# The third output-matrix unit of each MLP's last quarter computed by block products

## The chip, the cores and the metric

One Trainium2 chip, one core. The metric is the device time of one launch in microseconds (us), the median of several runs. The kernel has one long program: TensorE (PE) multiplies, VectorE (DVE), ScalarE (ACT) and GpSimd (POOL) prepare operands and take results, SyncE (SP) loads weights.

## The reference, cut to what matters

A first block (gated delta net, retention, a gated MLP) is followed by two layers of attention and a squared-relu MLP on a hidden state of 512 tokens by 1024 features, all in float32. The change touches the two MLPs of those layers and the norms behind them:

```
h = h + mix                                  # 512 x 1024
n = rms_norm(h, norm_mlp_g[i])               # over the 1024 features
h = h + relu(n @ w_in) ** 2 @ w_out          # w_in 1024 x 4096, w_out 4096 x 1024
# behind layer 0: rms_norm(h, norm_mix_g[1]), then n @ b_w_qkv
# behind layer 1: rms_norm(h, norm_final_g), the result
```

## The kernel before

**Tiles.** The hidden state is kept turned: `hT` holds 8 tiles of 128 features by 512 tokens. A weight unit is 256 columns of a weight matrix over 1024 rows (1 MB); its product with 8 operand tiles gives two tiles of output. Every number is split in a rounded part and a rest (`w_hi`, `w_lo`; `n_hi`, `n_lo`; `ff_hi`, `ff_lo`), and every product is three: hi by hi, hi by lo, lo by hi (`products`, lines 1063 to 1065). A plain unit is therefore 2 x 8 x 3 = 48 matmuls of 512 columns. SP loads a unit into one half of `raw` (line 898) as soon as the unit two before it has its rests; ACT makes its rounded part (`split_hi`, line 1895), DVE its rest (`split_lo`, line 1901).

**Quarters.** An MLP is done in four quarters m (0 to 3 in layer 0, 4 to 7 in layer 1) of 1024 inner features: four units of the input matrix, then four of the output matrix (units 0 to 3 of `p_dn[m]`), each of which is added to two tiles of `hT` (`residual_group`, line 3196): unit 0 to tiles 0 and 1, unit 1 to 2 and 3, unit 2, the third, to 4 and 5, unit 3 to 6 and 7.

**Block products.** The input units of quarters 1 to 3 are computed by a scheme of seven products of half-size blocks in place of eight (`block_tensor`, `piece_product`, lines 1500 to 1502): 7 x 4 x 3 = 84 matmuls of 256 columns. The pieces are A11, A12, A22, S2, S3, S1, S4 in this order; the S pieces are sums of weight blocks (made by `paired_sums`, `second_sum`, `fourth_sum`), the T factors are sums of operand blocks. In quarters 1, 2, 5 and 6 (`has_down`) the third output unit, called DOWN, is also done so. DVE then makes its weight sums behind the last input unit (`burst_vector`) and four operand sums in `scratch` (`down_sums`); ACT and DVE split these (`t_split_high`, `t_split_low`), and DVE adds the banks to tiles 4 and 5 in eight steps (`first_added`, `third_added`, `second_added`, `last_added`, lines 2141 to 2160), of which the steps wait for pieces S2, S3, S1 and S4. In quarters 3 and 7 all four output units are plain: `project` on PE, `rounds` on ACT, `residual` on DVE.

**The norms behind quarters 3 and 7** (n = 5 and n = 7). ACT reads the tiles of `hT` in three parts (tiles 0 to 3, 4 and 5, 6 and 7). For n = 5, `input_part` makes the rounded operands `n_hi` of a part (line 2232) and its squares in `scratch` (line 2223), and between part 0 and part 1 ACT splits the first weight unit of layer 1 (`next_split`). DVE makes the rests `n_lo` (`low`, line 2361), the rest of that weight unit (line 1901) and the residual additions. POOL adds the squares of the parts (`norm_pool`, lines 987, 989, 990), each step when the part's squares are there. For n = 7, the last, DVE multiplies the tiles by the norm's weights (`weighted`, line 2334) in place of the rests, and adds tile 6's squares to POOL's sum (line 2352) before it adds the last tile 7 (line 2343); then PE sums over features, DVE and ACT make the roots and scale the turned rows (`x_rows`), and SP stores them.

**What sets the order.** Each engine runs its own list in the order in which it is written. Engines wait for each other by counting semaphores. DVE's list behind quarter 3 is: rests of tiles 0 to 3, addition of tiles 4 and 5, rests of 4 and 5, rest of the next weight unit, additions and rests of 6 and 7. PE's first matmul of layer 1's projection waits for the rest of that weight unit.

Of the kernel before, what the change touches and what calls it, by code (L numbers as in the profile page):

```python
# [18 lines left out]
KD = D // P  # L19
# [186 lines left out]
def build(nc, t, out):  # L206
# [15 lines left out]
    with ctx:  # L222
# [543 lines left out]
        BLOCKS, DOWN = UNITS + 1, UNITS  # L766
        PIECES = [(name, u) for u in range(BLOCKS) for name in FACTORS]
        PIECE_AT = {piece: n for n, piece in enumerate(PIECES)}
# [3 lines left out]
        SPLITS = [(op, u) for u in range(UNITS) for op in ("A1", "S23", "S14")]  # L772
        SPLITS += [(op, DOWN) for op in ("T4", "T2", "A1", "S23", "T3", "S14", "T1")]
        SPLIT_AT = {op: n for n, op in enumerate(SPLITS)}
        T_SUMS = ("T1", "T3", "T2", "T4")
        SUM_AT = [3 * u for u in range(BLOCKS)]
        OPERANDS, SUMS = 4, KD + 4

        def has_down(m):
            return m % 4 in (1, 2)  # L780

        def counted(m, each, short, begin):

            layer, quarter = divmod(m, 4)
            return layer * (begin + 2 * each + short) + (begin + (quarter - 1) * each if quarter else 0)

# [5 lines left out]

        def pieces_before(m):
            return counted(m, len(PIECES), len(FACTORS) * UNITS, 0)

        def splits_before(m):

            return counted(m, len(SPLITS), 3 * UNITS, OPERANDS) + m // 4

        def sums_before(m):  # L800

            return counted(m, 3 * BLOCKS + len(T_SUMS), 3 * UNITS, SUMS)

        def kept_before(m):
            return counted(m, BLOCKS, UNITS, 0)

        PIECE_HI_ENDS = OPERANDS + 2 * len(SPLITS) + 3 * UNITS + 1

        def split_count(m, op):
            return splits_before(m) + SPLIT_AT[op] + 1  # L810

        def piece_split(eng, m, op, u, what):

            if op == "A22":
                eng.wait_ge({"hi": hi_ready, "lo": lo_ready}[what], unit_index(m, u) + 1)
            else:
                eng.wait_ge(at("piece_" + what), split_count(m, (op, u)))

        def piece_used(eng, m, piece):
            eng.wait_ge(at("piece_used"), pieces_before(m) + PIECE_AT[piece] + 1)  # L820

        def summed(eng, m, u, n):

            eng.wait_ge(at("sums_ready"), sums_before(m) + SUM_AT[u] + n)

# [43 lines left out]
        def kept(eng, m, u):  # L869
            eng.wait_ge(at("kept"), kept_before(m) + u + 1)  # L870

# [656 lines left out]
        def burst_tensor(pe, m):  # L1528
            if m % 4 == 1:
                pe.wait_ge(at("piece_lo"), splits_before(m))  # L1530
            for u in range(UNITS):
                block_tensor(pe, m, u)
# [479 lines left out]
        def operands_high(act, m):  # L2012

            act.wait_ge(w_used, p_in[m].u0 + 4)
            act.wait_ge(at("sums_ready"), sums_before(m) + KD)
            n0 = splits_before(m + 1) - OPERANDS
            for half in range(2):
                tiles = slice(4 * half, 4 * half + 4)
                done(act, act.activation(n_hi[:, tiles, :], n_whole[:, tiles, :], ACT.Copy), at("piece_hi"), n0 + half + 1)

        def operands_high_late(act, m):
            n0 = splits_before(m + 1) - OPERANDS
            act.wait_ge(at("sums_ready"), sums_before(m) + SUMS)
            act.wait_ge(at("piece_lo"), n0 + 2)
            for half in range(2):
                tiles = slice(KD + 4 * half, KD + 4 * half + 4)
                done(act, act.activation(ff_hi[:, tiles, :], t_tiles[:, 4 * half:4 * half + 4, :], ACT.Copy), at("piece_hi"), n0 + half + 3)

        def normed(dve, m, layer):

            for f in range(KD):
                done(dve, dve.scalar_tensor_tensor(n_whole[:, f, :], hT[:, f, :], input_weight((4, 6)[layer], f), rstd[:, :], ALU.mult, ALU.mult),
                     at("sums_ready"), sums_before(m) + f + 1)

        def operand_sums(dve, m):
            near, far = near_far(n_whole)
            n0 = sums_before(m) + KD
            done(dve, dve.tensor_tensor(t_parts[:, 0], near[:, :, LATER], near[:, :, EARLY], ALU.subtract), at("sums_ready"), n0 + 1)
            done(dve, dve.scalar_tensor_tensor(t_parts[:, 1], far[:, :, LATER], -1.0, t_parts[:, 0], ALU.mult, ALU.subtract), at("sums_ready"), n0 + 2)
            done(dve, dve.scalar_tensor_tensor(t_parts[:, 2], far[:, :, LATER], -1.0, near[:, :, LATER], ALU.mult, ALU.subtract), at("sums_ready"), n0 + 3)  # L2040
            done(dve, dve.tensor_tensor(t_parts[:, 3], t_parts[:, 1], far[:, :, EARLY], ALU.add), at("sums_ready"), n0 + 4)

        def operand_low(dve, m, n):

            n0 = splits_before(m + 1) - OPERANDS
            dve.wait_ge(at("piece_hi"), n0 + n + 1)
# [4 lines left out]
            done(dve, dve.tensor_tensor(lo, whole, hi.bitcast(F32), ALU.subtract), at("piece_lo"), n0 + n + 1)  # L2051

# [26 lines left out]
        def paired_sums(dve, m, u):  # L2079
# [47 lines left out]
        def first_kept(act, m, u):  # L2127

            piece_used(act, m, ("A11", u))
            done(act, act.activation(first_row(u), unit_banks(u)[0][:, EARLY], ACT.Copy), at("kept"), kept_before(m) + u + 1)  # L2130

# [25 lines left out]
        def last_added(dve, m, u):  # L2157
            piece_used(dve, m, ("S4", u))
            row = down_rows()[0][:, LATER]
            done(dve, dve.tensor_tensor(row, unit_banks(u)[0][:, LATER], row, ALU.add), bank_free, unit_group(m, u) + 3)  # L2160

        def down_sums(dve, m):

            n0 = sums_before(m) + 3 * BLOCKS
            t1, t3, t2, t4 = (t_whole(scratch, name) for name in T_SUMS)
# [5 lines left out]
        def t_split_high(act, m, name):  # L2171

            act.wait_ge(at("sums_ready"), sums_before(m) + 3 * BLOCKS + len(T_SUMS))
            if name == "T1":
# [154 lines left out]
        def last_norm_vector(dve):  # L2329
# [35 lines left out]
        def norm_vector(dve, n):  # L2365
# [266 lines left out]
        def mlp_scalar(act, layer):  # L2632
# [17 lines left out]
            for m in range(first + 1, first + 4):  # L2650
                burst_scalar(act, m)
                if has_down(m):
                    down_scalar(act, m)
            rounds(act, p_dn[first + 3], a_own, 0, split_hi, no_group)

        def down_scalar(act, m):
# [10 lines left out]
            split_hi(act, ph.u0 + 3, 1)  # L2667
            for op in PIECE_OF_OP:
                piece_high(act, m + 1, op, 0)

# [533 lines left out]
        def mlp_vector(dve, layer):  # L3204
# [517 lines left out]
```

## Time and profile before

| | |
|---|---|
| median of 3 runs | 1871.3 us (1871.23 to 1871.88) |
| span of the profiled execution, first to last instruction | 1869.4 us |
| busy PE, DVE, ACT, POOL | 99%, 71%, 50%, 5% |
| last chain | PE 94%, DVE 3%, ACT 1%, DMA 1% |
| granted TensorE clock | 0.999 on average |

The page gives the span of the profiled execution and no other time of it; the runs' median is 1.9 us above that span. A timeline row reads: start in us, length in us, engine, line, operation, output<-inputs, shapes, count; in brackets the idle time of the engine just before and what ended it. A merged row (x2, x4) has the time of all. Matmuls overlap: their pace is the distance of their starts, not their length.

### The profile page before, as it was taken

The page shows a single profiled execution, that of the slowest core. Times are in us where ns is not written, and L with a number is a line of the kernel's source. Part 1 is how long each engine was busy: PE and PEld are TensorE (multiplying, and loading weights), DVE is VectorE, ACT ScalarE, POOL GpSimd, SP SyncE. Part 2 cuts the span into 40 slices and gives each one's busy share as a digit, 9 for nine tenths or more (in the row PEclk, how much of TensorE's full clock was granted, in tenths as well). Part 3 has the DMA queues.
Part 4 walks back from the last instruction along what each step waited for, and adds up shares of the span by engine and source line. Part 5 has one row for each costly group of instructions (what it writes and reads, how often), then busy time and mean ns, then how long its engine had stood idle before and what let it go on. Part 6 is the DMA issues. An engine that isn't in the chain of part 4 may idle for free.

```text
span 1869.4 us, 28026 instructions
## 1 busy us (share of the span) xinstructions
PE 1857.1 (99%) x10531; PEld 1541.6 (82%) x10531; DVE 1329.9 (71%) x1824; ACT 931.1 (50%) x1190; POOL 101.9 (5%) x90
## 2 busy tenths in 40 slices
PE   9999999999999999999999999999999999999998
PEld 7788878888888887877889898988778788989897
DVE  7767774677357667556577898947788658789884
ACT  6392464555133344444543554545667744445462
POOL 0010021000000021000100000020110010000001
PEclk9999999999999999999999999999999999999999
DMA  7223122322322234222232223334232133233321
GB/s 242 90 91 123 40 68 68 109 93 68 112 90 94 76 100 140 68 78 68 93 101 97 93 95 109 98 108 147 88 105 71 60 101 104 81 105 99 105 90 68
DMA packets 146801, 179.31 MB, mean 96 GB/s; under 512 B 3582, under 2 KB 140670, under 8 KB 144257
## 3 DMA queue, kind: packets, MB, share of 16 engines
q1 hardware_dynamic: 143296, 160.44, 26.2%
q0 software_dynamic: 3104, 17.10, 2.9%
q8 instruction: 72, 1.18, 0.3%
q14 instruction: 41, 0.33, 0.1%
q10 hardware_dynamic: 288, 0.26, 0.0%
HBM read 173.48 MB, written 2.20 MB: 94 GB/s over the span
## 4 chain that ended last, share of the span: by engine, by line
PE 94%; DVE 3%; ACT 1%; DMA 1%; issue 0%; SPq 0%; DVEq 0%; ACTq 0%
PE bank L1063 23%; PE bank L1065 23%; PE bank L1064 23%; PE bank L1500 5%; PE bank L1501 5%; PE bank L1502 5%; PE bank L1191 2%; PE bank L1805 2%; PE bank L1787 1%; PE bank L1197 1%; PE bank L1676 1%; PE bank L1677 1%; PE bank L1678 1%; PE bank L1611 1%; PE bank L1664 1%; DVE w_lo L1901 0%
## 5 line engine op out<-in xcount | busy, mean ns | idle before, releaser
L1063 PE MATMUL bank<-n_hi,w_hi 128*128 128x512 f32 x1054 | 425.0, 403 | 1.4 <-DVE w_lo L1901 1.3
L1065 PE MATMUL bank<-n_hi,w_lo 128*128 128x512 f32 x1054 | 417.7, 396 | 0.0
L1064 PE MATMUL bank<-n_lo,w_hi 128*128 128x512 f32 x1054 | 416.6, 395 | 0.0
L1895 ACT ACTIVATE w_hi<-raw 128x2048 fp32r<-128x2048 f32 (+2 forms) x117 | 218.8, 1870 | 371.9 <-PE bank L1065 369.3
L1901 DVE TENSOR_TENSOR w_lo<-raw,w_hi 128x2048 fp32r<-128x2048 f32 (+2 forms) x123 | 275.7, 2242 | 112.2 <-ACT w_hi L1895 110.2
L1064 PE MATMUL bank<-ff_lo,w_hi 128*128 128x512 f32 x784 | 309.0, 394 | 0.0
L1065 PE MATMUL bank<-ff_hi,w_lo 128*128 128x512 f32 x720 | 286.2, 397 | 0.0
L1063 PE MATMUL bank<-ff_hi,w_hi 128*128 128x512 f32 x720 | 284.4, 395 | 0.6 <-DVE ff_lo L2200 0.6
L1063 PEld LDWEIGHTS bank<-n_hi,w_hi 128*128 128x128 f32 x1054 | 198.0, 188 | 53.9 <-issue 5.0
L1064 PEld LDWEIGHTS bank<-n_lo,w_hi 128*128 128x128 f32 x1054 | 198.1, 188 | 48.8 <-issue 2.9
L1065 PEld LDWEIGHTS bank<-n_hi,w_lo 128*128 128x128 f32 x1054 | 197.9, 188 | 47.0
L1064 PEld LDWEIGHTS bank<-ff_lo,w_hi 128*128 128x128 f32 x784 | 147.2, 188 | 36.7 <-issue 0.7
L1063 PEld LDWEIGHTS bank<-ff_hi,w_hi 128*128 128x128 f32 x720 | 135.1, 188 | 33.8 <-DVE ff_lo L2200 1.9
L1065 PEld LDWEIGHTS bank<-ff_hi,w_lo 128*128 128x128 f32 x720 | 135.1, 188 | 32.1
L3196 DVE TENSOR_TENSOR hT<-hT,bank 128x512 f32<-128x512 f32 (+1 forms) x94 | 64.6, 687 | 95.7 <-PE bank L1065 92.9
L1500 PE MATMUL bank<-ff_hi,w_hi 128*128 128x256 f32 x432 | 122.2, 283 | 0.0
L1501 PE MATMUL bank<-ff_lo,w_hi 128*128 128x256 f32 x432 | 122.0, 282 | 0.0
L1502 PE MATMUL bank<-ff_hi,w_lo 128*128 128x256 f32 x432 | 121.1, 280 | 0.0
L2062 ACT ACTIVATE w_hi<-consts 128x1024 fp32r<-128x1024 f32 x56 | 59.4, 1062 | 98.8 <-PE bank L1065 57.4
L1502 PEld LDWEIGHTS bank<-ff_hi,w_lo 128*128 128x128 f32 x432 | 82.1, 190 | 0.0
L1500 PE MATMUL bank<-n_hi,w_hi 128*128 128x256 f32 x288 | 81.5, 283 | 0.0
L1501 PE MATMUL bank<-n_lo,w_hi 128*128 128x256 f32 x288 | 81.4, 282 | 0.0
(455 smaller groups left out, 3015.2 us busy)
## 6 DMA issues: line engine op xcount, KB each, us to landing
raw<-in_mlp_w_in SPq DMA_DIRECT2D x32, 1024.0 KB, 5.4
raw<-in_mlp_w_out SPq DMA_DIRECT2D x32, 1024.0 KB, 5.1
raw<-in_w_up SPq DMA_DIRECT2D x22, 1024.0 KB, 5.1
raw<-in_w_units SPq DMA_DIRECT2D x14, 1024.0 KB, 4.8
raw<-in_a_w_qkv SPq DMA_DIRECT2D x12, 1024.0 KB, 5.1
raw<-in_b_w_qkv SPq DMA_DIRECT2D x12, 1024.0 KB, 5.2
b_bias<-bias_table POOLq DMA_DIRECT2D x16, 448.0 KB, 4.6
raw<-in_w_down SPq DMA_DIRECT2D x8, 768.0 KB, 4.6
```

The lines of the kernel that those rows point to most:

```text
L1063: nc.tensor.matmul(b[:, :], w_hi[:, j % 2, cols], hi, start=start, stop=False)
L1064: nc.tensor.matmul(b[:, :], w_hi[:, j % 2, cols], lo, start=False, stop=False)
L1065: return nc.tensor.matmul(b[:, :], w_lo[:, j % 2, cols], hi, start=False, stop=final)
L1191: ins = nc.tensor.transpose(b[:, i * P:(i + 1) * P], src(i), ident)
L1500: nc.tensor.matmul(b, w_hi_flat[:, cols], hi[:, k, :], start=k == 0, stop=False)
L1501: before = nc.tensor.matmul(b, w_hi_flat[:, cols], lo[:, k, :], start=False, stop=False)
L1502: ins = nc.tensor.matmul(b, w_lo_flat[:, cols], hi[:, k, :], start=False, stop=k == KD // 2 - 1)
L1805: ins = nc.tensor.matmul(b[:, :], b_v[:, head, k, :], b_at[:, head % 2, k, :], start=k == 0, stop=k == TOK - 1)
L1895: act.activation(w_hi[:, s, cols], raw[:, s, cols], ACT.Copy).then_inc(hi_ready, 1)
L1901: dve.tensor_tensor(w_lo[:, s, cols], raw[:, s, cols], w_hi[:, s, cols].bitcast(F32), ALU.subtract).then_inc(lo_ready, 1)
L2062: ins = act.activation(by_rows(places(w_hi_flat, op, u), op), source(m, op, u), ACT.Copy)
L3196: ins = dve.tensor_tensor(h, h, b[:, :].unsqueeze(1), ALU.add)
```

## The change

`has_down(m)` is now true for the quarters 3 and 7 too, so their third output unit becomes a DOWN unit of seven pieces, with weight sums, operand sums, splits and additions as in quarters 1, 2, 5 and 6. The next quarter's preparations, which follow there, are left out. ACT now waits, before part 0 of the norms 5 and 7, until piece S1 is used. DVE's addition of tiles 4 and 5 is the eight-step one, and the work on tiles 0 to 3 (rests for n = 5, weighting for n = 7), formerly ahead of the addition of tiles 4 and 5, stands between its fourth and its fifth step. The semaphore counts, formerly worked out by formulas, come from tables that are filled in the order of the work; this alone changes no instruction.

```diff
         def has_down(m):
-            return m % 4 in (1, 2)
+            return m % 4 > 0
...
+        def third_unit_added(dve, m, between):
+            first_added(dve, m, DOWN)
+            third_added(dve, m, DOWN)
+            between()
+            second_added(dve, m, DOWN)
+            last_added(dve, m, DOWN)
...
             def input_part(part):
                 residual_part(act, n, part)
+                if n == 5 and part == 0:
+                    piece_used(act, 3, ("S1", DOWN))
...
             for part in range(2):
                 residual_part(act, 7, part)
+                if part == 0:
+                    piece_used(act, 7, ("S1", DOWN))
                 squared(act, 7, part)
...
             own_splits(dve, ph, split_lo)
-            weighted(0, 4)
-            residual_group(dve, ph, ph.iters - 1, 0)
+            third_unit_added(dve, 7, lambda: weighted(0, 4))
             weighted(4, 6)
...
-                low(*PARTS[0])
+                if n != 5:
+                    low(*PARTS[0])
                 own_splits(dve, ph, split_lo, ...)
-                residual_group(dve, ph, ph.iters - 1, 0)
+                if n == 5:
+                    third_unit_added(dve, 3, lambda: low(*PARTS[0]))
+                else:
+                    residual_group(dve, ph, ph.iters - 1, 0)
                 low(*PARTS[1])
                 next_split(dve, n, split_lo, 0)
                 residual_group(dve, ph, ph.iters - 1, 1)
...
                 if has_down(m):
                     down_scalar(act, m)
-            rounds(act, p_dn[first + 3], a_own, 0, split_hi, no_group)
...
                 if has_down(m):
                     down_vector(dve, m)
-            residual(dve, p_dn[first + 3])
...
             piece_low(dve, m, "S14", DOWN)
             t_split_low(dve, m, "T1")
             split_lo(dve, ph.u0 + 3, 1)
+            if m % 4 == 3:
+                return
             first_added(dve, m, DOWN)
```

## Rows read from the trace of the kernel before

**Rows 1.** The page: busy us and share; granted clock in 40 slices.

```profile
PE 1857.1 (99%) x10531; PEld 1541.6 (82%) x10531; DVE 1329.9 (71%) x1824; ACT 931.1 (50%) x1190; POOL 101.9 (5%) x90
...
PEclk9999999999999999999999999999999999999999
```

**Rows 2.** Timeline of PE: first matmuls of three units, plain ones before and behind.

```profile
1236.00 0.40 PE L1063 MATMUL bank<-ff_hi,w_hi 128*128 128x512 f32 x1
...
1258.40 0.40 PE L1063 MATMUL bank<-n_hi,w_hi 128*128 128x512 f32 x1
...
1834.90 0.39 PE L1063 MATMUL bank<-ff_hi,w_hi 128*128 128x512 f32 x1
```

**Rows 3.** Timeline of PE: first matmul of quarter 6's DOWN and unit 3.

```profile
1750.77 0.28 PE L1500 MATMUL bank<-ff_hi,w_hi 128*128 128x256 f32 x1
...
1760.94 0.44 PE L1063 MATMUL bank<-ff_hi,w_hi 128*128 128x512 f32 x1
```

**Rows 4.** Timeline of PE and DVE; waits of PE (us, times, longest).

```profile
1736.66 0.50 PE L1063 MATMUL bank<-ff_hi,w_hi 128*128 128x512 f32 x1 [0.65 <-DVE ff_lo L2200]
...
1732.66 1.23 DVE L2088 TENSOR_TENSOR consts<-raw 128x1024 f32<-128x1024 f32 x1 [2.54 <-DMA raw<-in_mlp_w_out]
...
PE bank L1063 <- DVE ff_lo L2200: 0.6, 1, 0.6
```

**Rows 5.** Timeline of ACT and DVE in and behind quarter 6's DOWN unit.

```profile
1752.46 0.38 ACT L2130 ACTIVATE kept_rows<-bank 128x256 f32<-128x256 f32 x1 [0.79 <-PE bank L1502]
...
1758.46 2.29 DVE L1901 TENSOR_TENSOR w_lo<-raw,w_hi 128x2048 fp32r<-128x2048 f32 x1 [0.59 <-ACT w_hi L1895]
...
1761.97 0.69 DVE L2143 TENSOR_TENSOR hT<-hT,kept_rows 128x512 f32<-128x512 f32 x1
...
1762.70 0.42 DVE L2147 TENSOR_TENSOR kept_rows<-bank,kept_rows 128x256 f32<-128x256 f32 x1
...
1767.79 0.42 DVE L2160 TENSOR_TENSOR hT<-bank,hT 128x256 f32<-128x256 f32 x1
```

**Rows 6.** Timeline of ACT, DVE and POOL, norm 5 behind quarter 3.

```profile
1238.23 3.00 ACT L2232 ACTIVATE n_hi<-hT,par 128x512 fp32r<-128x512 f32 x4
...
1240.63 3.12 DVE L2361 SCALAR_TENSOR_TENSOR n_lo<-hT,par,n_hi 128x512 fp32r<-128x512 f32 x4
...
1241.26 1.92 ACT L2223 ACTIVATE scratch<-hT 128x2048 f32<-128x2048 f32 x1
...
1249.43 1.48 ACT L2232 ACTIVATE n_hi<-hT,par 128x512 fp32r<-128x512 f32 x2
...
1250.26 1.54 DVE L2361 SCALAR_TENSOR_TENSOR n_lo<-hT,par,n_hi 128x512 fp32r<-128x512 f32 x2 [2.08 <-ACT n_hi L2232]
...
1251.83 2.29 DVE L1901 TENSOR_TENSOR w_lo<-raw,w_hi 128x2048 fp32r<-128x2048 f32 x1
...
1252.15 4.24 POOL L989 TENSOR_TENSOR scratch<-scratch 128x1024 f32<-128x1024 f32 x1 [6.14 <-ACT scratch L2223]
```

**Rows 7.** Timeline, norm 7; line 2334 by itself (min/median/max ns).

```profile
1839.14 2.62 POOL L987 TENSOR_TENSOR scratch<-scratch 128x1024 f32<-128x1024 f32 x1 [327.03 <-ACT scratch L2223]
...
1848.39 2.40 POOL L989 TENSOR_TENSOR scratch<-scratch 128x1024 f32<-128x1024 f32 x1 [6.63 <-ACT scratch L2223]
...
1850.87 1.29 POOL L990 TENSOR_TENSOR scratch<-scratch 128x512 f32<-128x512 f32 x1
...
1857.57 0.69 DVE L2343 TENSOR_TENSOR hT<-hT,bank 128x512 f32<-128x512 f32 x1 [3.35 <-PE bank L1065]
...
L2334 DVE TENSOR_SCALAR h_w<-hT,par x8: 486/487/2508, 1839.5 to 1858.3; 128x512 f32<-128x512 f32 x8
```

**Rows 8.** Timeline of POOL, and the last chain in time, in norm 2.

```profile
694.24 2.71 POOL L996 TENSOR_TENSOR a_k<-a_k,scratch 128x1024 f32<-128x1024 f32 x1 [2.00 <-ACT scratch L2223]
...
694.71 2.80 DVE a_stage L2417
```

**Rows 9.** Waits of PE: the longest one.

```profile
PE bank L1813 <- DVE g_S L3618: 1.1, 1, 1.1
```

More of the change, by code:

```diff
@@ L766, in build @@
         BLOCKS, DOWN = UNITS + 1, UNITS
-        PIECES = [(name, u) for u in range(BLOCKS) for name in FACTORS]
-        PIECE_AT = {piece: n for n, piece in enumerate(PIECES)}
         PLACE = {"A11": 0, "A12": 1, "A22": 2, "S2": 4, "S3": 5, "S1": 6, "S4": 7}
@@ L771, in build @@
         PIECE_OF_OP = {"A1": ("A11", "A12"), "A22": ("A22",), "S23": ("S2", "S3"), "S14": ("S1", "S4")}
-        SPLITS = [(op, u) for u in range(UNITS) for op in ("A1", "S23", "S14")]
-        SPLITS += [(op, DOWN) for op in ("T4", "T2", "A1", "S23", "T3", "S14", "T1")]
-        SPLIT_AT = {op: n for n, op in enumerate(SPLITS)}
         T_SUMS = ("T1", "T3", "T2", "T4")
-        SUM_AT = [3 * u for u in range(BLOCKS)]
-        OPERANDS, SUMS = 4, KD + 4
+        OPERANDS = 4
+        DOWN_SPLITS = ("T4", "T2", "A1", "S23", "T3", "S14", "T1")
         def has_down(m):
-            return m % 4 in (1, 2)
-        def counted(m, each, short, begin):
-            layer, quarter = divmod(m, 4)
-            return layer * (begin + 2 * each + short) + (begin + (quarter - 1) * each if quarter else 0)
+            return m % 4 > 0
         def unit_index(m, u):
@@ L791, in unit_group, with count @@
             return p_in[m].g0 + u if u < UNITS else p_dn[m].g0 + 2
[L793 to L810, printed above, removed]
+        piece_count, split_count, sum_count, kept_count = {}, {}, {}, {}
+        def count(table, *key):
+            table[key] = len(table) + 1
+        for layer in range(2):
+            for n in range(KD + 4):
+                count(sum_count, 4 * layer, "operand", n)
+            if layer:
+                count(split_count, 4, "output_begun")
+            for n in range(OPERANDS):
+                count(split_count, 4 * layer, "operand", n)
+            for m in range(4 * layer + 1, 4 * layer + 4):
+                for u in range(BLOCKS if has_down(m) else UNITS):
+                    count(kept_count, m, u)
+                    for name in FACTORS:
+                        count(piece_count, m, name, u)
+                    for op in DOWN_SPLITS if u == DOWN else ("A1", "S23", "S14"):
+                        count(split_count, m, op, u)
+                    for n in (1, 2, 3):
+                        count(sum_count, m, u, n)
+                if has_down(m):
+                    for name in T_SUMS:
+                        count(sum_count, m, name)
+        PIECE_HI_ENDS = split_count[4, "output_begun"]
         def piece_split(eng, m, op, u, what):
@@ L816, in piece_split @@
             else:
-                eng.wait_ge(at("piece_" + what), split_count(m, (op, u)))
+                eng.wait_ge(at("piece_" + what), split_count[m, op, u])
         def piece_used(eng, m, piece):
-            eng.wait_ge(at("piece_used"), pieces_before(m) + PIECE_AT[piece] + 1)
+            eng.wait_ge(at("piece_used"), piece_count[(m,) + piece])
         def summed(eng, m, u, n):
-            eng.wait_ge(at("sums_ready"), sums_before(m) + SUM_AT[u] + n)
+            eng.wait_ge(at("sums_ready"), sum_count[m, u, n])
         def places_free(eng, m, op, u):
@@ L869, in kept @@
         def kept(eng, m, u):
-            eng.wait_ge(at("kept"), kept_before(m) + u + 1)
+            eng.wait_ge(at("kept"), kept_count[m, u])
         def unit_rows(u):
@@ L1529, in burst_tensor @@
             if m % 4 == 1:
-                pe.wait_ge(at("piece_lo"), splits_before(m))
+                pe.wait_ge(at("piece_lo"), split_count[m - 1, "operand", OPERANDS - 1])
             for u in range(UNITS):
@@ L2014, in operands_high @@
             act.wait_ge(w_used, p_in[m].u0 + 4)
-            act.wait_ge(at("sums_ready"), sums_before(m) + KD)
-            n0 = splits_before(m + 1) - OPERANDS
+            act.wait_ge(at("sums_ready"), sum_count[m, "operand", KD - 1])
             for half in range(2):
                 tiles = slice(4 * half, 4 * half + 4)
-                done(act, act.activation(n_hi[:, tiles, :], n_whole[:, tiles, :], ACT.Copy), at("piece_hi"), n0 + half + 1)
+                done(act, act.activation(n_hi[:, tiles, :], n_whole[:, tiles, :], ACT.Copy), at("piece_hi"), split_count[m, "operand", half])
         def operands_high_late(act, m):
-            n0 = splits_before(m + 1) - OPERANDS
-            act.wait_ge(at("sums_ready"), sums_before(m) + SUMS)
-            act.wait_ge(at("piece_lo"), n0 + 2)
+            act.wait_ge(at("sums_ready"), sum_count[m, "operand", KD + 3])
+            act.wait_ge(at("piece_lo"), split_count[m, "operand", 1])
             for half in range(2):
                 tiles = slice(KD + 4 * half, KD + 4 * half + 4)
-                done(act, act.activation(ff_hi[:, tiles, :], t_tiles[:, 4 * half:4 * half + 4, :], ACT.Copy), at("piece_hi"), n0 + half + 3)
+                done(act, act.activation(ff_hi[:, tiles, :], t_tiles[:, 4 * half:4 * half + 4, :], ACT.Copy), at("piece_hi"), split_count[m, "operand", 2 + half])
         def normed(dve, m, layer):
@@ L2032, in normed @@
                 done(dve, dve.scalar_tensor_tensor(n_whole[:, f, :], hT[:, f, :], input_weight((4, 6)[layer], f), rstd[:, :], ALU.mult, ALU.mult),
-                     at("sums_ready"), sums_before(m) + f + 1)
+                     at("sums_ready"), sum_count[m, "operand", f])
         def operand_sums(dve, m):
             near, far = near_far(n_whole)
-            n0 = sums_before(m) + KD
+            n0 = sum_count[m, "operand", KD] - 1
             done(dve, dve.tensor_tensor(t_parts[:, 0], near[:, :, LATER], near[:, :, EARLY], ALU.subtract), at("sums_ready"), n0 + 1)
@@ L2043, in operand_low @@
         def operand_low(dve, m, n):
-            n0 = splits_before(m + 1) - OPERANDS
-            dve.wait_ge(at("piece_hi"), n0 + n + 1)
+            dve.wait_ge(at("piece_hi"), split_count[m, "operand", n])
             half = slice(4 * (n % 2), 4 * (n % 2) + 4)
@@ L2050, in operand_low @@
                              (t_tiles[:, half, :], ff_hi[:, spare, :], ff_lo[:, spare, :]))
-            done(dve, dve.tensor_tensor(lo, whole, hi.bitcast(F32), ALU.subtract), at("piece_lo"), n0 + n + 1)
+            done(dve, dve.tensor_tensor(lo, whole, hi.bitcast(F32), ALU.subtract), at("piece_lo"), split_count[m, "operand", n])
         def unit_loaded(eng, v):
@@ L2129, in first_kept @@
             piece_used(act, m, ("A11", u))
-            done(act, act.activation(first_row(u), unit_banks(u)[0][:, EARLY], ACT.Copy), at("kept"), kept_before(m) + u + 1)
+            done(act, act.activation(first_row(u), unit_banks(u)[0][:, EARLY], ACT.Copy), at("kept"), kept_count[m, u])
         def down_rows():
@@ L2171, in t_split_high @@
         def t_split_high(act, m, name):
-            act.wait_ge(at("sums_ready"), sums_before(m) + 3 * BLOCKS + len(T_SUMS))
+            act.wait_ge(at("sums_ready"), sum_count[m, T_SUMS[-1]])
             if name == "T1":
@@ L2667, in down_scalar @@
             split_hi(act, ph.u0 + 3, 1)
-            for op in PIECE_OF_OP:
-                piece_high(act, m + 1, op, 0)
+            if m % 4 < 3:
+                for op in PIECE_OF_OP:
+                    piece_high(act, m + 1, op, 0)
         def burst_scalar(act, m):
```

8 lines of the change are left out of this document (4 added, 4 removed).

## The prediction, written before the change was built or run

> **What bounds the kernel now.** I read the page first: PE is busy 99% of the span and its clock is at the full level, 2.4 GHz, in every slice [rows 1]. So time can be won only by fewer PE cycles, and every wait that is put on PE costs in full. Then the timeline of PE around the touched places. In quarter 3 the third plain unit starts at 1236.00 and the first matmul of layer 1's projection at 1258.40, with no idle time between [rows 2]: two units, 22.40 us, 11.20 each. Quarter 7's third unit starts at 1834.90 [rows 2]. A DOWN unit in quarter 6 takes 1760.94 - 1750.77 = 10.17 us [rows 3]. Then the other engines behind both places, because the change hands them more work just before PE needs their results.
>
> **What it removes.** 48 matmuls of 512 columns become 84 of 256: 11.20 - 10.17 = 1.03 us per quarter, 2.06 us in two. This is all there is to win, 0.11% of the span. The 0.2% that tells a change of this kernel from none is 3.7 us, out of reach on the fast side.
>
> **What it adds ahead of the unit.** DVE's weight sums now stand before the last rests of the inner features, and wait for the weights: 2.54 us in quarter 6 [rows 4]. PE then waited for `ff_lo`. It was idle 0.65; with the 0.40 of the matmul before, starts lay 1.05 apart in place of 0.23, and the first matmul behind took 0.50 for 0.40: 0.9 us lost. But that is the only one of four such quarters with idle time [rows 4]; a wait below 0.17 us would hide in the 0.40 of a matmul. I take 0.1 us per quarter and keep 0.9 as its upper end. Four operand sums, the splits, and the S sums cost nothing else: the same lists run behind the same PE work in quarter 6, and the 10.17 us contain what they cost.
>
> **What is late behind quarter 3.** Times from here on are in us behind DOWN's first matmul, 0.
> - DVE: the rest of unit 3's weights starts at 1758.46 - 1750.77 = 7.69; the first four additions end at 1762.70 + 0.42 - 1750.77 = 12.35 [rows 5].
> - ACT: a piece is 12/84 of 10.17, 1.45 us, so S1 is done at 8.72. A signal of this kind took 1752.46 - (1750.77 + 1.45) = 0.24 us [rows 5]. The new wait thus ends at 8.96. Queued behind it are four rounded tiles (3.00) and the squares (1.92) [rows 6], to 13.9. Then the next weights' rounded part, also 1.92, to 15.9, which is early enough.
> - DVE's four rests, 3.12 together or 0.78 each [rows 6], start at 12.4 and would end at 15.5.
> - POOL starts to add squares at 14.0, within the third rest (14.0 to 14.7). What then happens stands in the trace of norm 2: POOL's addition of the same size came at 694.24, during one vector operation on two SBUF tensors; the next one, started at 694.71, took 2.80 us in place of 0.76, and ended 0.56 behind POOL's end at 696.95 [rows 8]. The other way round, POOL's addition at 1252.15 took 4.24 us for 2.40, as DVE's split of weights had begun at 1251.83 [rows 6, 7]. So each waits for the other's whole instruction. Here POOL goes at 14.7, ends at about 17.0, and the fourth rest ends at 17.55, not 15.5: +2.05.
> - The last four additions are 0.42 + 0.69 + 0.69 + 0.42 [rows 5] with 0.03 between them: to 19.9.
> - ACT's tiles 4 and 5 start at 20.0; DVE's rests of them end 1251.80 - 1249.43 = 2.37 later [rows 6], at 22.35; the weights' rest takes 2.29, to 24.7.
> - PE ends unit 3 at 10.17 + 0.04 + 11.20 = 21.4 and needs that rest: idle to 24.75, and 0.1 for the first matmul, as above.
>
> Before, PE got there at 22.40. Net: 0.1 + 24.75 + 0.1 - 22.40 = **+2.55 us**. Without the meeting of POOL and DVE: +0.5. With no wait at all: 0.1 + 21.4 - 22.4 = -0.9. Layer 1's later waits: its first operands 6 and 7 are needed 36 matmuls (8.4 us) behind that start, and come about 5 us behind it; I take 0.
>
> Of the meeting, the Trainium skill, "SBUF — State Buffer", section "SBUF: two separate sides", says that the port pair which VectorE and GpSimd share is an exclusive lock for a whole instruction, taken also by a vector operation with two SBUF inputs against a GpSimd one that reads SBUF. The rows of norm 2 agree. It speaks against this change, because before it POOL's additions fell into gaps of DVE, and now they meet a full list.
>
> **What is late at the end (quarter 7).** The same list up to 8.96. ACT squares at once, to 10.9; POOL starts at 11.0 and runs 2.6 [rows 7], to 13.65. DVE's third addition has two SBUF inputs and would start at 1761.97 - 1750.77 = 11.2 [rows 5]; blocked, it ends at about 14.15, not 11.9: +2.25. The fourth ends at 14.6. Four weightings, 0.49 each alone (one of the eight took 2.51, started during POOL's addition [rows 7]), 2.1 in all, to 16.7. Last additions to 19.05. Squares of tiles 4 and 5 (1.07, half as many as a 128x2048 row and its start) to 20.2; POOL's additions 2.40 and 1.29 [rows 7] with about 0.5 between and before them, to 24.4, the weighting of tile 6 locked out meanwhile; DVE's addition of tile 6's squares, 0.7, to 25.2. Only then tile 7 is added. Before, this was at 1857.57 - 1834.90 = 22.67 [rows 2, 7]. Everything behind it is unchanged. Net: 0.1 + 25.2 - 22.67 = **+2.65 us**. Without the first lock: +0.4. With no wait: PE ends at 21.4, tile 7's addition 0.27 behind it as before: -0.9.
>
> **Sum.** 2.55 + 2.65 = +5.2 us on the span, 1869.4 + 5.2 = 1874.6. The profiled execution shows no more than its span; the runs' median lies 1.9 above it, and I leave that as it is: 1871.3 + 5.2 = **1876.5 us**.
>
> **The rivals.**
> - *All of it is hidden (faster).* The waits of ACT and DVE end before PE needs them. Two times -0.9: 1869.5. For it: in quarters 1, 2, 5 and 6 longer lists are hidden. Against it: there unit 3 is followed by pieces prepared earlier, here by a weight rest that stands at the end of DVE's list; even without locks I find it 1.2 us late. 5%.
> - *The lists are late, but POOL and DVE don't meet.* If POOL's addition fell between instructions, or DVE went first: 0.5 + 0.4 = +0.9, 1872.2. The gaps decide: in quarter 7 POOL comes 0.2 us ahead of the addition that it blocks. 15%.
> - *One meeting only:* 0.5 + 2.65 or 2.55 + 0.4, about +3.1, 1874.4. 20%.
> - *The idle time also costs clock (more slower).* PE would be idle 3.3 us behind quarter 3 and 3.8 us near the end, against 1.1 us at the longest before [rows 9], where the clock stayed full [rows 1]. If it fell to 1.2 GHz, a stretch as long as the idle one would run at half pace: half of 3.3, and some of the 4 us of transposes at the end, +2 to +3, 1879. No row shows such a fall before the last instructions. 15%.
> - *The waits for weights repeat* as in quarter 6, twice 0.8 more: 1878.1. In the range of the forecast.
>
> Beside the fourth rival: the Trainium skill, "TensorE: Matmul & The Clock Gate", section "Part 1: The HAM clock gate", holds that an idle TensorE drops to 1.2 GHz and is brought back by work. No run here shows it for idle stretches of this length; by it the fourth rival's time would come out.
>
> **How the numbers follow.** Forecast, both meetings at full clock: 45%, 1875.2 to 1878.3 by its own terms. The range to 8 in 10 reaches from 1872.0 (the rival without meetings, nearly) to 1879.2 (clock). Faster by over 0.2% has no mechanism: 1%. Slower by over 0.2%, above 1875.0: the forecast, the clock's case, and part of the single meeting: 63%. The same: 36%.
>
> **What would show it.** Right: PE idle about 3.3 us ahead of the first line-1063 matmul of layer 1, released by DVE's line 1901; one vector operation of 2.5 to 3 us during each of POOL's first additions (a rest, line 2361, in norm 5; line 2143 in norm 7); tile 7's last addition released not by PE but by POOL's sum; DOWN units of 10.2 us. Wrong: no idle time of PE ahead of layer 1, or POOL's additions at 2.4 us beside vector operations at 0.69 to 0.76. If the locks are there and the total is still near 1872, the error is in where the lists end.

## The result and the profile after

| | before | after |
|---|---|---|
| median of 4 runs each | 1871.6 us | 1880.75 us (1879.75 to 1881.9) |
| ratio | | 1.0046, 95% interval 1.0032 to 1.0060 |
| span of the profiled execution | 1869.4 us | 1877.9 us |

The change costs 9.2 us. The forecast was +5.2 with a range to 1879.2; the result lies 1.5 above the range. The profiled execution is 8.5 longer, and that difference can be placed. The page after, as in [rows 1]: busy time of PE and POOL, and the granted clock by fortieths of the span.

```profile
PE 1862.2 (99%) x10603; PEld 1549.7 (83%) x10603; DVE 1369.3 (73%) x1864; ACT 944.3 (50%) x1206; POOL 101.9 (5%) x90
...
PEclk9999999999999999999999999999999999999998
```

The shares tell nothing of the loss: PE is busy 99% as before. A first sign is the mean granted clock, 0.996 in this execution (0.995 to 0.998 in the four) where before had 0.999.

**Quarter 3.** Timelines of DVE and then POOL of the kernel after (start, duration, engine, line, operation, shape, then in brackets idle time and releaser). DOWN's first matmul is at 1236.25 here.

```profile
1248.65 5.15 DVE L2366 SCALAR_TENSOR_TENSOR n_lo<-hT,par,n_hi 128x512 fp32r<-128x512 f32 x4
...
1255.74 0.42 DVE L2155 TENSOR_TENSOR hT<-bank,hT 128x256 f32<-128x256 f32 x1
1257.09 1.54 DVE L2366 SCALAR_TENSOR_TENSOR n_lo<-hT,par,n_hi 128x512 fp32r<-128x512 f32 x2 [0.92 <-ACT n_hi L2236]
1258.66 2.29 DVE L1899 TENSOR_TENSOR w_lo<-raw,w_hi 128x2048 fp32r<-128x2048 f32 x1
```

```profile
1250.31 2.94 POOL L985 TENSOR_TENSOR scratch<-scratch 128x1024 f32<-128x1024 f32 x1 [336.06 <-ACT scratch L2225]
```

The four rests took 5.15, where they took 3.12 before [rows 6]. POOL's addition lies inside them, and ends at 1253.25. All that follows on DVE is 2.03 later, down to the weight rest that PE needs. PE's own timeline there:

```profile
1257.46 0.39 PE L1063 MATMUL bank<-ff_hi,w_lo 128*128 128x512 f32 x1
1261.00 0.50 PE L1061 MATMUL bank<-n_hi,w_hi 128*128 128x512 f32 x1 [3.16 <-DVE w_lo L1899]
1261.34 0.40 PE L1062 MATMUL bank<-n_lo,w_hi 128*128 128x512 f32 x1
...
1262.68 0.63 PE L1061 MATMUL bank<-n_hi,w_hi 128*128 128x512 f32 x1
1263.11 0.63 PE L1062 MATMUL bank<-n_lo,w_hi 128*128 128x512 f32 x1
...
1265.67 0.41 PE L1062 MATMUL bank<-n_lo,w_hi 128*128 128x512 f32 x1
1265.92 0.39 PE L1063 MATMUL bank<-n_hi,w_lo 128*128 128x512 f32 x1
```

The first matmul of layer 1 starts 24.75 behind DOWN's, released by the weight rest; 3.16 us of PE are idle. Then comes what the prediction's sum did not have. From 1262.68 to 1265.67 seven matmuls start 0.43 apart, not 0.23, and last 0.63, not 0.40: 7 x 0.19, and 0.17 on the one ahead of them, 1.5 us. That is the lower clock level, 1.2 GHz. The rows of stretches say the same (us, busy time and count of PE, PEld, DVE, ACT, POOL, then the granted clock):

```profile
1236.00:1261.00 25.00, 21.85 (x134) 19.09 (x132) 22.47 (x25) 14.31 (x14) 4.97 (x2) 1.00 0.27 85
1261.00:1266.00 5.00, 5.00 (x15) 3.94 (x16) 3.98 (x5) 3.43 (x4) 4.92 (x5) 0.66 0.67 216
```

While PE is idle the row shows a full clock; it is lower only behind it. The page's fortieths, 47 us each, show 9 in every one but the last: a fall of 3.4 us (1262.28 to 1265.67) cannot be seen there.

**The end (quarter 7).** Timelines of DVE, POOL and PE after. DOWN starts at 1839.13.

```profile
1850.33 2.78 DVE L2138 TENSOR_TENSOR hT<-hT,kept_rows 128x512 f32<-128x512 f32 x1
...
1859.83 2.16 DVE L2340 TENSOR_SCALAR h_w<-hT,par 128x512 f32<-128x512 f32 x1
1863.19 0.69 DVE L2357 TENSOR_TENSOR scratch<-scratch 128x512 f32<-128x512 f32 x1 [1.21 <-POOL scratch L988]
1863.92 0.69 DVE L2348 TENSOR_TENSOR hT<-hT,bank 128x512 f32<-128x512 f32 x1
...
1868.43 0.17 DVE L2359 TENSOR_REDUCE r_cols<-bank 128x4 f32<-128x8 f32 x1 [3.30 <-PE bank L1873]
```

```profile
1850.16 2.41 POOL L985 TENSOR_TENSOR scratch<-scratch 128x1024 f32<-128x1024 f32 x1 [333.79 <-ACT scratch L2225]
...
1859.33 2.38 POOL L987 TENSOR_TENSOR scratch<-scratch 128x1024 f32<-128x1024 f32 x1 [6.76 <-ACT scratch L2225]
```

```profile
1864.03 1.84 PE L1869 MATMUL bank<-consts,scratch 128*128 128x1 f32 x8 [3.33 <-DVE scratch L2357]
...
1866.62 1.71 PE L1873 MATMUL bank<-consts,scratch 128*128 128x1 f32 x8
1868.19 5.73 PE L1189 MATMUL bank<-consts,h_w 128*128 128x128 f32 x28
```

The addition of two SBUF tensors takes 2.78 (0.69 alone), as POOL came 0.17 ahead of it; the weighting of tile 6 takes 2.16 (0.49 alone). Tile 7's addition waits for the chain behind POOL's sums, not for PE, and starts 24.79 behind DOWN. PE is idle for 3.33, and the clock is low again: eight sums take 1.84 and 1.71, where before and the kernels below that keep the clock show 0.95 to 1.08. Stretches of after, then one of before:

```profile
1863.00:1864.00 1.00, 0.00 (x0) 0.00 (x0) 0.77 (x2) 0.00 (x0) 0.11 (x1) 0.52 0.00 0
1864.00:1869.40 5.40, 5.37 (x26) 5.40 (x27) 1.45 (x5) 0.97 (x3) 0.00 (x0) 0.50 0.00 0
```

```profile
1857.30:1860.30 3.00, 2.71 (x24) 2.47 (x23) 1.28 (x3) 0.63 (x1) 0.00 (x0) 1.00 0.00 0
```

Here the clock falls while PE is still idle, 2.3 us behind the end of its last matmul (1860.70), and stays low for about 10 us, until 1873.3.

**The 8.5 us.** Delay of after against before at matching places: 0.25 at quarter 3's third unit; 2.60 at layer 1's first matmul (1261.00 - 1258.40); 4.23 at quarter 7's (1839.13 - 1834.90), 1.5 of what is added since then being clock; 6.35 at tile 7's addition (1863.92 - 1857.57), thus 2.1 for the end's list; 6.73 at the first of the sums (1864.03 - 1857.30); 8.24 at the reduction of the sums (1868.43 - 1860.19). From the first of the sums to the end of the span after takes 13.87 us (1877.9 - 1864.03) and before 12.10 (1869.4 - 1857.30). So only 0.3 is added behind the reduction (8.5 - 8.24), though the 28 transposes take 5.73 in place of 3.25: the slow sums cost, the slow transposes hardly.

### The profile page after: what moved, and what is told of

It is laid out like the page before. It is cut to its first block, busy times and chain, and to the rows that moved or that the text cites. A ratio compares the mean times of both kernels' runs of the same rounds, so it can differ in the third digit from the quotient of the medians.

```text
span 1877.9 us, 28246 instructions
## 1 busy us (share of the span) xinstructions
PE 1862.2 (99%) x10603; PEld 1549.7 (83%) x10603; DVE 1369.3 (73%) x1864; ACT 944.3 (50%) x1206; POOL 101.9 (5%) x90
## 4 chain that ended last, share of the span: by engine, by line
PE 93%; DVE 4%; ACT 2%; issue 0%; DMA 0%; POOL 0%; POOLq 0%; DVEq 0%; ACTq 0%; SPq 0%
PE bank L1061 22%; PE bank L1063 22%; PE bank L1062 22%; PE bank L1498 5%; PE bank L1500 5%; PE bank L1499 5%; PE bank L1189 2%; PE bank L1803 1%; PE bank L1785 1%; PE bank L1195 1%; PE bank L1674 1%; DVE w_lo L1899 1%; PE bank L1675 1%; PE bank L1676 1%; PE bank L1609 1%; PE bank L1662 1%
## 5 line engine op out<-in xcount | busy, mean ns | idle before, releaser
L1899 DVE TENSOR_TENSOR w_lo<-raw,w_hi 128x2048 fp32r<-128x2048 f32 (+2 forms) x121 | 271.1, 2241 | 106.8 <-ACT w_hi L1893 104.8
L1062 PE MATMUL bank<-ff_lo,w_hi 128*128 128x512 f32 x752 | 296.9, 395 | 0.0
L1063 PE MATMUL bank<-ff_hi,w_lo 128*128 128x512 f32 x688 | 272.8, 397 | 0.0
L1061 PE MATMUL bank<-ff_hi,w_hi 128*128 128x512 f32 x688 | 272.2, 396 | 0.4 <-DVE ff_lo L2202 0.4
L1062 PEld LDWEIGHTS bank<-ff_lo,w_hi 128*128 128x128 f32 x752 | 141.2, 188 | 34.4 <-issue 0.7
L1061 PEld LDWEIGHTS bank<-ff_hi,w_hi 128*128 128x128 f32 x688 | 129.1, 188 | 33.1 <-DVE ff_lo L2202 2.4
L1498 PE MATMUL bank<-ff_hi,w_hi 128*128 128x256 f32 x456 | 128.9, 283 | 0.0
L1500 PE MATMUL bank<-ff_hi,w_lo 128*128 128x256 f32 x456 | 128.4, 281 | 0.0
L1499 PE MATMUL bank<-ff_lo,w_hi 128*128 128x256 f32 x456 | 128.3, 281 | 0.0
L2057 ACT ACTIVATE w_hi<-consts 128x1024 fp32r<-128x1024 f32 x60 | 63.7, 1062 | 101.0 <-PE bank L1063 57.5
L1499 PEld LDWEIGHTS bank<-ff_lo,w_hi 128*128 128x128 f32 x456 | 86.1, 189 | 0.3
L1498 PEld LDWEIGHTS bank<-ff_hi,w_hi 128*128 128x128 f32 x456 | 85.4, 187 | 0.3
```

The lines of the kernel that those rows point to most:

```text
L1061: nc.tensor.matmul(b[:, :], w_hi[:, j % 2, cols], hi, start=start, stop=False)
L1062: nc.tensor.matmul(b[:, :], w_hi[:, j % 2, cols], lo, start=False, stop=False)
L1063: return nc.tensor.matmul(b[:, :], w_lo[:, j % 2, cols], hi, start=False, stop=final)
L1498: nc.tensor.matmul(b, w_hi_flat[:, cols], hi[:, k, :], start=k == 0, stop=False)
L1499: before = nc.tensor.matmul(b, w_hi_flat[:, cols], lo[:, k, :], start=False, stop=False)
L1500: ins = nc.tensor.matmul(b, w_lo_flat[:, cols], hi[:, k, :], start=False, stop=k == KD // 2 - 1)
```

## Experiments

The medians of before beside them were 1871.9 (e1 to e4), 1872.0 (e5 to e8) and 1872.2 (e9).

**e1 and e2: one quarter alone.**

```diff
-            return m % 4 > 0
+            return m % 4 in (1, 2) or m in THIRD     # e1: THIRD = (3,)   e2: THIRD = (7,)
```

The other quarter keeps its lists of before.

> Only quarter 3 has its third output unit by block products, quarter 7 is as before. Theory (late lists, POOL and DVE locking each other out, and a clock that falls because PE then idles): layer 1 begins some 2.5 us later and its first matmuls at half clock add 1.5 to 2, so +3.8 to +4.4: 1875.7. Rival (the loss is a loss of the end of the kernel alone, and what is lost in quarter 3 is taken up by waits in layer 1): 1871.5. PE idle 3.2 us ahead of the projection's first matmul as in the changed kernel.

> Only quarter 7 has it. Theory: tile 7's last addition 2.3 to 2.7 us later, and the last sums and transposes at half clock another 2 to 3: +4.5 to +5.5: 1876.6. Rival (the locks alone, clock of no account): +2.5, 1874.1. If the two parts are independent, the losses of this run and of the one with quarter 3 alone add up to 9.2.

e1: 1874.9 (1873.65 to 1875.9), ratio 1.0015 [1.0006, 1.0024]. e2: 1875.7, ratio 1.0020 [1.0011, 1.0029]. So both quarters lose, as the forecast has it: +3.0 and +3.8, against the forecast's +2.55 and +2.65 without clock; with clock I had expected +3.8 to +4.4 and +4.5 to +5.5, and both came out lower. In e2's profile POOL's first addition stretches DVE's to 2.79, PE is idle 3.34, and the sums take 1.64 and 1.71, as in the change. e1's profiled execution surprised: the same idle stretch, and no fall of the clock.

```profile
1261.03 0.50 PE L1063 MATMUL bank<-n_hi,w_hi 128*128 128x512 f32 x1 [3.17 <-DVE w_lo L1901]
1261.37 0.40 PE L1064 MATMUL bank<-n_lo,w_hi 128*128 128x512 f32 x1
...
1262.54 0.40 PE L1063 MATMUL bank<-n_hi,w_hi 128*128 128x512 f32 x1
1262.77 0.39 PE L1064 MATMUL bank<-n_lo,w_hi 128*128 128x512 f32 x1
```

Its 11 times seem to fall into two groups, four at 1873.65 to 1874.03 (the profiled one, 1873.81, among them) and seven at 1874.66 to 1875.94, though a gap as wide, 0.7, lies within the upper one. Their medians are 1.85 apart. That fits executions without and with the fall. Only one is profiled, but every run has its mean granted clock: 1.000 three times and 0.999 in the lower group, 0.998 to 0.999 in the upper; 3.4 us at half clock would lower the mean of 1872 us by 0.0009. So the figures agree with it, as finely as three digits can, though before's runs spread over the same 0.998 to 1.000. The medians of e1 and e2 add up to 6.9, the whole change costs 9.2; the spans add up better: 2.6 + 4.5 (1873.9 - 1869.4), and the 1.5 that e1's profile doesn't have, make 8.6 for 8.5.

**e3: the same lists, PE kept busy.** 12 matmuls of 512 columns on data at hand stand ahead of each of PE's two waits (layer 1's first unit, shown, and the sums at the end); their results are overwritten.

```diff
+            for _ in range(12):
+                nc.tensor.matmul(proj_bank[0][:, :], ones_r[:, :], FF_HI[0], start=True, stop=True)
+            pe.wait_ge(bank_free, ph.g0 + 1)
...
+            for _ in range(12):
+                nc.tensor.matmul(b[:, :], ones_r[:, :], FF_HI[0], start=True, stop=True)
             pe.wait_ge(norm_two, ADDED[7] + 1)
```

> The changed kernel, with 12 matmuls of 512 columns that nobody reads on PE in each of its two idle stretches (2.8 of 3.2 and of 3.3 us). Theory: the clock stays at 2.4 GHz, the lists and locks stay: what is left is the +5.2 that was predicted, 1876.8, and both stretches behind the idle time run at full pace. Rival (the clock is not what makes the last 4 us): 1880.7 as the changed kernel, or more.

1876.1 (1875.5 to 1877.4), ratio 1.0022 [1.0013, 1.0031], span 1873.7. PE at the end:

```profile
1858.70 2.69 PE L1869 MATMUL bank<-ff_hi,ones_r 128*128 128x512 f32 x11
1861.91 1.05 PE L1872 MATMUL bank<-consts,scratch 128*128 128x1 f32 x8 [0.52 <-DVE scratch L2360]
1862.82 0.63 PE L1189 MATMUL bank<-consts,h_w 128*128 128x128 f32 x4
1863.35 1.05 PE L1876 MATMUL bank<-consts,scratch 128*128 128x1 f32 x8
```

Both sums take 1.05, and from their start to the end of the span it is 11.8 us (1873.7 - 1861.91), not 13.9. Nothing of the lists has changed: layer 1 starts at 1260.96. So filler work on PE takes 4.7 us off the changed kernel (1880.75 to 1876.1, from two sets of runs; 4.9 by each one's distance to before, 9.2 and 4.2). The mean granted clock of its 11 runs is 0.998 to 1.000, as before's. In the spans it is 4.2: 1.5 at layer 1, 2.1 at the end (13.87 - 11.79), and some 0.5 in quarter 6, where the wait for `ff_lo`, 0.41 idle in the kernel after, isn't there in this execution. What is left, +4.2 in the median, is the lists.

**e6: quarter 3 alone, with the 12 matmuls.**

> Only quarter 3 by block products, as in the changed kernel, and 12 matmuls on PE that nobody reads in the idle stretch ahead of layer 1. The executions with quarter 3 alone fell in two groups, 1873.65 to 1874.03 and 1874.66 to 1875.94. Clock theory: the idle stretch costs clock in some executions and not in others; with PE kept busy only the lower group is left, 1873.9 with a spread under 1. Rival (the groups come from something else): two groups again, median 1874.9.

1873.1 (1872.5 to 1873.4), ratio 1.0007 [0.9998, 1.0016]. The 1.85 between two groups is gone: 11 times within 0.9. With the granted clocks it is the strongest sign that e1's upper group is clock. The level is 0.8 below what I expected, 0.7 below e1's lower group. The profiled execution has no wait for `ff_lo` in quarter 6, where the kernel before lost 0.9: the load of weights that DVE's sums wait for kept DVE 1.58 us, and 2.57 in e1. That is enough for the 0.7; why the load comes earlier, I did not test.

**e4: POOL's first addition later**, so that it doesn't meet the work of tiles 0 to 5.

```diff
+            if n == 5:
+                pool.wait_ge(lo_ready, p_qkv.u0 + 1)
+            if n == 7:
+                pool.wait_ge(bank_free, p_dn[7].g0 + 5)
             done(pool, pool.tensor_tensor(two, two, scratch[:, 2:4, :], ALU.add), at("norm_four"), i + 1)
```

> The changed kernel, but POOL's first addition of squares waits: in norm 5 until the rest of the next weight unit is made, in norm 7 until tiles 4 and 5 are added. Theory: in quarter 3 the fourth rest takes 0.75 and PE's idle time falls from 3.2 to about 1.2, too short for the clock to fall: -3.7; in quarter 7 line 2138 takes 0.69 but POOL's sum is then the last: tile 7 about 1.1 earlier: in all 1875.9. Rival (the lists are late without the locks): both idle stretches stay above 3 us, 1880.7.

1877.6 (1875.8 to 1879.0), ratio 1.0028 [1.0017, 1.0039]: 1.7 worse than expected. DVE and PE in norm 5:

```profile
1249.22 3.12 DVE L2370 SCALAR_TENSOR_TENSOR n_lo<-hT,par,n_hi 128x512 fp32r<-128x512 f32 x4
...
1261.85 3.56 DVE L2370 SCALAR_TENSOR_TENSOR n_lo<-hT,par,n_hi 128x512 fp32r<-128x512 f32 x2 [0.92 <-ACT n_hi L2240]
1265.45 1.67 DVE L2408 TENSOR_TENSOR scratch<-scratch 128x512 f32<-128x512 f32 x1
```

```profile
1259.55 0.50 PE L1065 MATMUL bank<-n_hi,w_hi 128*128 128x512 f32 x1 [1.15 <-DVE w_lo L1903]
...
1272.91 0.50 PE L1065 MATMUL bank<-n_hi,w_hi 128*128 128x512 f32 x1 [1.44 <-DVE w_lo L1903]
```

The first half went as the lock says: rests 3.12 again, the idle stretch 1.15 in place of 3.16, and a full clock behind it. But POOL's three additions then met the next rests (3.56 for 1.54) and a sum (1.67 for 0.69), and the next unit's weights came 1.44 late. At the end DVE's addition took 0.69 as expected, but PE still waited 2.9 for POOL's sums, and the clock was at half behind that. A lock that is put off is paid elsewhere; a list has to have room for it.

**e7: the first addition nearly left out.** In norms 5 and 7 POOL adds 16 columns in place of 1024, so part of the squares is missing from the sums.

```diff
+            if n in (5, 7):
+                done(pool, pool.tensor_tensor(scratch[:, 0:2, 0:8], scratch[:, 0:2, 0:8], scratch[:, 2:4, 0:8], ALU.add), ...)
+            else:
...
```

> The changed kernel, but POOL's first addition of squares in norms 5 and 7 covers 8 columns of each tile in place of 512 (the rest of the squares of tiles 2 and 3 is left out of those norms). Lock theory: in norm 5 the four rests take 3.1 in place of 5.15 and PE idles 1.2 ahead of layer 1 in place of 3.2, clock kept: quarter 3 costs +0.5; in norm 7 line 2138 takes 0.69 in place of 2.78 and tile 7 comes 2.2 earlier, PE idle 1.3, clock kept: +0.4. In all 1872.8. Rival (the order of the list, not the lock, makes the lateness): idle stretches stay near 3 us, 1879 to 1880.7.

1874.0 (1872.3 to 1875.05), ratio 1.0011 [1.0002, 1.0020]; DVE in norm 5, and at the end:

```profile
1248.88 3.11 DVE L2369 SCALAR_TENSOR_TENSOR n_lo<-hT,par,n_hi 128x512 fp32r<-128x512 f32 x4
...
1846.96 0.69 DVE L2141 TENSOR_TENSOR hT<-hT,kept_rows 128x512 f32<-128x512 f32 x1
...
1854.37 2.19 DVE L2343 TENSOR_SCALAR h_w<-hT,par 128x512 f32<-128x512 f32 x1
```

Without the first addition the rests take 3.11 and the SBUF addition 0.69: both meetings are causes, not company. Locked only by the second addition is the weighting at the end, 2.19. PE is idle 1.15 and 1.30. The clock is full behind the first; at the end of this execution it fell in the 28 transposes:

```profile
1860.92 4.88 PE L1192 MATMUL bank<-consts,h_w 128*128 128x128 f32 x28
```

where before shows 3.25. That fall cost nothing here: from the first sum to the end of the span it is 11.87 us (1870.5 - 1858.63), before 12.10. And this execution, at 1872.3, is the fastest of the eleven and 0.5 below what was expected; the median is 1.2 above it because six of the eleven lie at 1874.04 to 1875.05, all with a mean granted clock of 0.998, and the other five at 1872.26 to 1873.10 with 0.998 to 1.000. That points to clock again, but where it fell in those six no profile shows.

**e5 and e8: another order.** The six additions that read a bank come first, under POOL's addition, and the two between SBUF tensors last. e5 does it in quarter 7, with quarter 3 as before; weightings come after the additions.

```diff
...
+            own_dve(dve, dve.tensor_tensor(third_row(u), y[:, LATER], first_row(u), ALU.add))
+            own_dve(dve, dve.tensor_tensor(row, y[:, :], row, ALU.add))
+            third_added(dve, m, u)
...
+            own_dve(dve, dve.tensor_tensor(row[:, LATER], z[:, LATER], row[:, LATER], ALU.add))
+            own_dve(dve, dve.tensor_tensor(below, z[:, :], below, ALU.add))
...
+            own_dve(dve, dve.tensor_tensor(row[:, LATER], x[:, LATER], row[:, LATER], ALU.add))
+            own_dve(dve, dve.tensor_tensor(halves(row), halves(row), twice(first_row(u)), ALU.add))
+            done(dve, dve.tensor_tensor(halves(below), halves(below), twice(third_row(u)), ALU.add), ...)
```

> Only quarter 7 by block products, in another order: DVE takes its six additions from banks first and the two additions with two SBUF inputs last, then weights tiles 0 and 1, adds tile 6, weights 2 and 3, adds the squares, adds tile 7 and weights 4 to 7. Lock theory: POOL's first addition then lies beside instructions that read a bank, none of which it stretches; tile 7 is added as soon as PE is done (about 0.3 us behind its last matmul), PE idles less than 1 us, the clock stays. What is left is the shorter unit: 0.9 below the kernel before, 1871.0. Rival (the eight additions and the weightings are too long for the time whatever their order): tile 7 over 1.5 us late, 1873.5 or more.

e8 does it in both. In norm 5 the weight rest moves ahead of the tiles' rests (`next_split(dve, n, split_lo, 0)` before `low(0, 1)`), the additions of tiles 6 and 7 stand between those rests, and on ACT the squares stand behind the first rounded tile and the second weight unit's rounded part ahead of the norm's sum. So e8 changes more than the order of the eight additions.

> Both quarters by block products, both orders changed. Quarter 7 as in the run with banks first. Behind quarter 3: ACT squares tiles 0 to 3 right behind piece S1, DVE takes the six additions from banks first, then makes the next weights' rest ahead of all rests of tiles, and adds tiles 6 and 7 between those rests, where POOL adds squares; the second weight unit is split ahead of the sum. Lock theory: POOL's three additions lie beside bank reads or cost little, the weights' rest is ready before PE ends unit 3: no idle time ahead of layer 1, 0.9 us gained per quarter: 1870.1, below both kernels. Rival (DVE has too much to do between DOWN and layer 1's second unit in any order): a wait of 1 to 2 us at layer 1's first or second unit, 1871.5 to 1872.5.

> The same kernel as e8_both_reordered (third unit in quarters 3 and 7, six additions from banks ahead of the two between SBUF tensors, lists reordered), timed again to learn whether its 1.3 us below the kernel before is real. Theory: with both locks gone the change keeps 1.0 us of gain per quarter less small waits, so it stays 1.0 to 1.6 us below the kernel before (ratio 0.9992 to 0.9995), PE with no idle stretch over 0.3 us ahead of layer 1. Rival: e8's difference was scatter between two groups of runs, and the two kernels come out within 0.5 us.

e5: 1871.3, ratio 0.9998 [0.9989, 1.0007]. So quarter 7 alone went from +3.8 to no loss. e8: 1870.7, 0.9994 [0.9985, 1.0003]. e9, e8's kernel again: 1870.7, 0.9992 [0.9983, 1.0001]. DVE and POOL of e8 in norm 5:

```profile
1248.24 0.42 DVE L2142 TENSOR_TENSOR kept_rows<-bank,kept_rows 128x256 f32<-128x256 f32 x1
1248.70 0.42 DVE L2167 TENSOR_TENSOR hT<-bank,hT 128x256 f32<-128x256 f32 x1
1249.16 0.69 DVE L2168 TENSOR_TENSOR hT<-bank,hT 128x512 f32<-128x512 f32 x1
1249.88 0.42 DVE L2170 TENSOR_TENSOR hT<-bank,hT 128x256 f32<-128x256 f32 x1
...
1252.30 2.29 DVE L1899 TENSOR_TENSOR w_lo<-raw,w_hi 128x2048 fp32r<-128x2048 f32 x1 [0.54 <-ACT w_hi L1893]
```

```profile
1248.04 2.42 POOL L985 TENSOR_TENSOR scratch<-scratch 128x1024 f32<-128x1024 f32 x1 [333.14 <-ACT scratch L2242]
```

Four additions lie beside POOL's 2.42, at 0.42 and 0.69 like those without it. The lock isn't gone: two of the later rests take 3.75 for 1.54 and two weightings at the end 3.35 for 1.01, beside POOL's second and third additions; but there nothing on PE waits for them. PE's longest wait in the whole kernel is again 1.1, as in [rows 9]. At the end tile 7's addition waits for PE:

```profile
1857.09 0.69 DVE L2381 TENSOR_TENSOR hT<-hT,bank 128x512 f32<-128x512 f32 x1 [0.79 <-PE bank L1063]
```

Behind this the clock fell too, in e8's and in e9's profiled execution, without an idle stretch over 0.31 us. PE of e8:

```profile
1859.92 4.94 PE L1189 MATMUL bank<-consts,h_w 128*128 128x128 f32 x28 [0.31 <-DVE h_w L2373]
```

In e5, with the same list for quarter 7, they took 3.28. The end is no longer for it: 12.28 us from the first sum in e8 (1869.1 - 1856.82), 12.33 in e5 (1869.0 - 1856.67).

This is the version that keeps a little of the gain: 1.3 and 1.6 us under the kernel before in two separate comparisons. Both intervals just reach past 1, so the medians alone do not settle it. The profiles agree with them: counted from a wait of PE that all have (848.29 before, 849.01 in e8, 848.65 in e9), the rest of the span is 1.0 and 1.6 us shorter. It is likely and not settled; about 10 us under the change as made is settled.

## Why the prediction was wrong

*Right.* The unit: those of quarters 3 and 7 took 10.18 each (10.17 taken). Both meetings of POOL and DVE, with their sizes: rests 5.15 (3.12 + 2.05 forecast), the addition 2.78 (about 2.95). Where the lists end: layer 1's matmul at 24.75 behind DOWN's (24.75), tile 7's addition at 24.79 (25.2). The idle stretch ahead of layer 1, 3.16 (3.3), and its releaser. e4 and e7 show that these meetings make most of the idle time: in e7 layer 1 starts 22.73 behind DOWN's first matmul (1259.21 - 1236.48). The rule in the Trainium skill, "SBUF — State Buffer", section "SBUF: two separate sides", names an operation with two SBUF inputs as one that takes the lock; e8's additions with a bank as one input, unstretched, agree with it.

*Wrong.* The step that failed is the term for clock: the sum holds nothing for it and keeps PE at the full level, and "the idle time also costs clock" was a rival at 15% with +2 to +3. In the profiled execution the clock cost 1.5 at layer 1 and 2.1 at the end, 3.6; in the medians e3 takes 4.9 away, and the lists that the sum does hold are left at +4.2 (5.2 forecast). With 3.6 the forecast would have read 1880.1. Two readings led there. I took "the longest wait before is 1.1, and the clock stayed full" as a mild sign against a fall, though it says nothing of 3 us; what no row shows should have got a chance near one half, and the end of the range, 1879.2, cut off the upper part of that rival's own +2 to +3. The rival's price rested on low stretches as long as the idle ones, which no row showed: behind 3.16 us of idle time 3.4 us were slow, behind 3.33 about 10. And I counted the loss at the end on the transposes; the sixteen small sums, which stand on the path to the reduction, paid 1.5 of it (8.24 at the reduction less 6.73 at the first sum), the transposes 0.3.

*Beside it.* Quarter 6's wait for `ff_lo`, 0.65 us idle before [rows 4], was 0.41 after, 0.95 in e4 and none in e3 and e6. It can move the time of a variant by about 1, which fits e3's and e6's distance of 0.7 to 0.8 below what was expected. The clock fell with PE idle for 3.16 and 3.33 us after, stayed full behind 3.17 in e1, and fell behind 0.31 in e8. The rule that the prediction cites from the Trainium skill, "TensorE: Matmul & The Clock Gate", section "Part 1: The HAM clock gate", agrees with the profile after; what e1's and e8's show doesn't follow from the sentence cited.

*Open.* What decides whether an idle stretch of 3.2 us costs clock, and whether the small matmuls at the end do; and 1.3 us between 4.9 in the medians and 3.6 in the profiles, of which 0.5 may be quarter 6's wait. e1 and e2 add up to 6.9 and the whole change costs 9.2; how often the clock falls in each kernel isn't known, and it may be that.

## What to carry to other kernels

Before work is placed ahead of something PE waits for, mark on its list each VectorE operation with two SBUF operands and each GpSimd one, and put under GpSimd's those that read a bank: the change costs 9.2 us with one order of the lists and nothing with another. When a sum leaves PE idle for 3 us, where it never was, price it twice, with the clock full and with half pace behind it (here 3.4 us among large matmuls, about 10 among small ones), keep both in the range, and count the half pace on the work that stands on the path to the end.

## What was not expected of the hardware

- One idle stretch, 3.16 and 3.17 us in two profiled executions, was followed by 3.4 us at 1.2 GHz in one and by none in the other; at the end of e7, e8 and e9, amid small matmuls, it fell without an idle stretch over 1.30, 0.31 and 0.31 us, and in before, e1, e3, e5 and e6 it did not fall there.
- At layer 1 the slower pace begins 1.3 us behind the first matmul (1261.00 to 1262.28), not with the idle time; at the end it begins 2.3 us into the idle time. The 28 transposes at half pace (4.88 to 4.94 us for 3.25) added nothing to the time in e7 and at most 0.3 in e8 and e9.
- VectorE's bank-reading additions (0.42 and 0.69) run beside GpSimd's of 2.4 us without loss, in each of e5's and e8's lists. Its weightings, from SBUF to SBUF with one tensor as input, are stretched (2.16 us for 0.49).
